# Two feed-forward blocks in two phases, with ten of eleven down units formed from seven products of block sums

## What is computed

```python
def swiglu(x, w1, w3, w2):
    return (jax.nn.silu(x @ w1) * (x @ w3)) @ w2

h = h + 0.5 * swiglu(rmsnorm(h, ffn1_norm[l]), ffn1_w1[l], ffn1_w3[l], ffn1_w2[l])   # FFN1
...   # pooling mixer and retention ("MIX", w_in, w_out)
h = h + 0.5 * swiglu(rmsnorm(h, ffn2_norm[l]), ffn2_w1[l], ffn2_w3[l], ffn2_w2[l])   # FFN2
```

## Time and profile before

| | us |
|---|---|
| three runs | 841.17, 840.43, 839.87 (median 840.43) |
| span of the profiled execution, first to last instruction | 837.8 |
| PE busy | 828.7 (99%) |
| DVE, ACT, POOL busy | 639.9, 447.6, 88.1 |

### The profile page before, as it was taken

One profiled execution on the slowest core, in us unless ns is written; L12 is line 12 of the kernel. 1 busy time (PEld: TensorE's weight loads), 2 busy tenths in 40 slices (PEclk: granted clock), 3 DMA queues, 4 the chain that ended last, 5 costly groups with the idle time before them and its releaser, 6 DMA issues.

```text
span 837.8 us, 13770 instructions
## 1 busy us (share of the span) xinstructions
PE 828.7 (99%) x5313; PEld 731.7 (87%) x5315; DVE 639.9 (76%) x791; ACT 447.6 (53%) x564; POOL 88.1 (11%) x93
## 2 busy tenths in 40 slices
PE   8999999999999999999999999999999999999996
PEld 6888888888988888888888899999998988888895
DVE  5786766667967587676667779897775898998897
ACT  6555444546324554544444756784425655665664
...
GB/s 242 317 240 210 184 196 205 167 201 159 243 158 144 151 206 259 239 180 197 204 194 169 132 220 156 132 172 223 159 154 198 141 201 201 150 200 212 189 175 51
DMA packets 119970, 157.73 MB, mean 188 GB/s; under 512 B 4429, under 2 KB 104173, under 8 KB 119805
## 3 DMA queue, kind: packets, MB, share of 16 engines
...
HBM read 154.42 MB, written 1.07 MB: 186 GB/s over the span
## 4 chain that ended last, share of the span: by engine, by line
PE 98%; DMA 1%; POOL 0%; ACTq 0%; DVE 0%; issue 0%; POOLq 0%; DVEq 0%
PE wk L1722 30%; PE acc L1844 20%; PE wk L1691 18%; PE wk L1730 16%; PE acc L1821 7%; PE wk L2171 1%; PE acc L2135 1%; PE acc L1738 1%; DMA x<-in_x 1%; PE acc L1691 1%; PE acc L2150 1%; PE wk L2233 1%; PE wk L2235 0%; PE acc L1857 0%; PE acc L2196 0%; PE wk L2031 0%
## 5 line engine op out<-in xcount | busy, mean ns | idle before, releaser
L1722 PE MATMUL wk<-xhl,w_hi 128*128 128x512 f32 x1104 | 268.9, 391 | 0.0
L1040 DVE TENSOR_TENSOR w_lo<-raw,w_hi 128x2048 fp32r<-128x2048 f32 x83 | 190.0, 2289 | 63.9 <-ACT w_hi L493 62.8
L1722 PEld LDWEIGHTS wk<-xhl,w_hi 128*128 128x128 f32 x1104 | 202.5, 188 | 38.9 <-issue 0.2
L493 ACT ACTIVATE w_hi<-raw 128x2048 fp32r<-128x2048 f32 x83 | 158.0, 1904 | 0.0
L1730 PEld LDWEIGHTS wk<-xhl,w_lo 128*128 128x128 f32 x1104 | 145.5, 191 | 8.0
L1730 PE MATMUL wk<-xhl,w_lo 128*128 128x256 f32 x1104 | 147.9, 282 | 0.0
L486 ACT ACTIVATE w_hi<-raw 128x2048 fp32r<-128x2048 f32 x55 | 104.6, 1910 | 51.6 <-PE wk L1691 29.9
L1023 DVE TENSOR_TENSOR w_lo<-raw,w_hi 128x2048 fp32r<-128x2048 f32 x48 | 110.2, 2300 | 21.3 <-ACT w_hi L486 21.1
L1844 PE MATMUL acc<-w_hi,hhl 128*128 128x512 f32 x480 | 119.4, 391 | 0.0
L1691 PE MATMUL wk<-xhl,w_hi 128*128 128x256 f32 x608 | 108.6, 286 | 0.0
L1844 PEld LDWEIGHTS acc<-w_hi,hhl 128*128 128x128 f32 x480 | 88.2, 188 | 17.1
...
## 6 DMA issues: line engine op xcount, KB each, us to landing
raw<-in_ffn_w SPq DMA_DIRECT2D x65, 1024.0 KB, 5.4
raw<-in_w_in SPq DMA_DIRECT2D x24, 1024.0 KB, 6.8
raw<-in_w_ffn_in SPq DMA_DIRECT2D x22, 1024.0 KB, 5.1
raw<-in_w_ffn_out SPq DMA_DIRECT2D x11, 1024.0 KB, 4.9
raw<-in_w_out SPq DMA_DIRECT2D x8, 1024.0 KB, 4.9
...
raw<-in_cmp_w_k SPq DMA_DIRECT2D x2, 1024.0 KB, 5.5
```

The costliest lines, as they stand in the source:

```text
L493: nc.scalar.activation(w_hi[:, s], raw[:, s], ACT.Copy).then_inc(hi_done, 1)
L1040: nc.vector.tensor_tensor(w_lo[:, s], raw[:, s], w_hi[:, s].bitcast(F32), ALU.subtract) \
L1722: mm = nc.tensor.matmul(bank, wh[:, c, cols], xhl[:, c].rearrange("p n t -> p (n t)"), start=c == 0, stop=False, skip_group_check=True)
```

## The change

FFN1 and FFN2 are done in two phases: first all 22 A and B units, then the 11 R units. The hidden values of ten steps are kept (`h_store`, in `arena`, and part of `mhl`) until then. The loops are written out.

For ten of the eleven R units the product of a 2 x 2 block of hidden values (two token tiles by two chunks of 128) and a 2 x 2 block of weights (two chunks by two halves of 512 columns) is formed from seven products of sums of blocks in place of eight products of blocks. Each of the seven has three passes of 512 columns, so PE does 21 matmuls in place of 24 for such a unit. They need four sums of hidden blocks for each step (`hidden_sums`: four POOL instructions of 128 x 128) and four sums of weight blocks for each unit (`folded_sums`: four POOL instructions of 128 x 512). The hidden store so has seven blocks in place of four: ACT and DVE cast and subtract 896 elements in place of 512. A unit's weights are seven blocks of 512 in place of four, in a ring of twelve (`ring_hi`, `ring_lo`): three blocks of the raw weights (`blocks_hi`, `blocks_lo`) and four sums (`sums_hi_part`, `sums_lo_part`, two at a time), 3584 elements in place of 2048 for ACT and for DVE. The sums of the units 2 and on lie where `xhl` lay, so POOL waits for the end of the first phase with them.

The seven products are summed over the units in seven or eight banks, four of `acc` and four of `wk`. At the end of the FFN they are combined (`folded_start` and `folded_corner` on DVE, three copies on ACT, two additions on POOL in `corner`). The gate's multiplication by `rstd_b` is left out; the per-token factor is put on at the end with `scale_t`. The loads of the MIX tables move from POOL's queue at the start to ACT's queue in the second phase, the bias loads on POOL and the clearing of `blk` (before FFN2) to the end of FFN2's sums.

```diff
+FB, RING = 512, 12
+FOLDED = FI - 1
+ITEMS = 7
+A_S1, A_S2, A_S3, A_S4, A_12, A_22, A_11 = range(ITEMS)
+PRODUCTS = ((A_12, 0), (A_S4, 2), (A_11, 4), (A_S3, 5), (A_S1, 6), (A_S2, 7), (A_22, 1))
+PAIRS = ((5, 6, 7, 2, 3, 4, 0, 1, 8, 9), (2, 0, 1, 3, 4, 5, 6, 7, 8, 9))
+IN_ARENA = 8
...
-        xhl = sb("xhl", [P, DC, 2, T], F32R)
+        xhl = nc.alloc_sbuf_tensor_at("xhl", [P, DC, 2, T], F32R, offset=XHL_AT)
+        sums_x23 = nc.alloc_sbuf_tensor_at("sums_x23", [P, 2, UNIT], F32, offset=XHL_AT)
...
+        weight_sums = [sqf, carve(56, UNIT), sums_x23[:, 0], sums_x23[:, 1]]
...
+
+        def h_pair(j):
+            return h_store[:, j] if j < IN_ARENA else mhl_pairs[:, j - IN_ARENA]
+
+        def product_bank(b):
+            return acc[:, b] if b < 4 else wk[:, b - 4]
...
+                if u is not None and sums_before(u):
+                    sp.wait_ge(w_sums, sums_before(u))
...
+                for p in range(FOLDED):
+                    j = PAIRS[f][p]
+                    unit(base + 2 * FI + p, r2[:, 2 * j:2 * j + 2, :], 2)
...
-                def h_hi(i, w2_before, dst=hh):
+                def h_hi(i):
                     act.wait_ge(h_out, i + (n0 + 1))
-                    if w2_before is not None:
-                        act.wait_ge(unit_done, w2_before)
-                    nc.scalar.activation(dst[:, 0:2], k_n(h_s, 2), ACT.Copy).then_inc(hh_out, 1)
-
-                a_part(0, base + 1)
+                    if i < FOLDED:
+                        act.wait_ge(h_sums, FOLDED * f + i + 1)
+                        nc.scalar.activation(h_pair(i)[:, 0], h_all[:, 0:ITEMS * P], ACT.Copy).then_inc(hh_out, 1)
+                    else:
+                        nc.scalar.activation(hh[:, 0:2], k_n(h_s, 2), ACT.Copy).then_inc(hh_out, 1)
...
+                def blocks_hi(p):
+
+                    u = base + 2 * FI + p
+                    act.wait_ge(raw_in[u % SLOTS], raw_count(u))
+                    ring_free(p, 2)
+                    for b, n, count in ring_parts(base, p, 0, 3):
+                        cast = nc.scalar.activation(ring_hi[:, b * FB:(b + count) * FB],
+                                                    raw[:, u % SLOTS, n * FB:(n + count) * FB], ACT.Copy)
+                    cast.then_inc(hi_done, 1)
+
+                def sums_hi_part(p, j):
+
+                    act.wait_ge(w_sums, 2 * (FOLDED * f + p) + j + 1)
+                    ring_free(p, 4 + 2 * j)
+                    for b, n, count in ring_parts(base, p, 3 + 2 * j, 2):
+                        cast = nc.scalar.activation(ring_hi[:, b * FB:(b + count) * FB],
+                                                    weight_sums[p % 4][:, (2 * j + n) * FB:(2 * j + n + count) * FB], ACT.Copy)
+                    cast.then_inc(sums_hi, 1)
...
+                h_hi(0)
+                for i in range(1, FI):
+                    a_part(i)
+                    if i < FI - 1:
+                        hi(base + 2 * i + 3)
+                    else:
+                        sums_hi_part(0, 0)
                     tanh(i)
-                    hi_in_loop(i, base, 2)
-                    b_part(i, i * 3 + (base + 1))
-                    hi_in_loop(i, base, 3)
-                    h_hi(i, i * 3 + (base + 2))
-                    hi_in_loop(i, base, 4)
-
-                a_part(FI - 1, base + 3 * FI - 3)
-                tanh(FI - 1)
+                    if i == FI - 1:
+                        sums_hi_part(0, 1)
+                    b_part(i)
+                    if i < FI - 2:
+                        hi(base + 2 * i + 4)
+                    else:
+                        blocks_hi(i - (FI - 2))
+                    h_hi(i)
+                for p in range(1, FOLDED):
+                    if p > 1:
+                        blocks_hi(p)
+                    sums_hi_part(p, 0)
+                    sums_hi_part(p, 1)
+                    if p == 5 and f == 0:
+                        act.wait_ge(unit_done, base + 2 * FI + 3)
+                        act.dma_start(table, a["c_table"]).then_inc(tables_in, 16)
+                        act.dma_start(pool_ws, a["pool_w"][0].rearrange("g k n -> k g n")).then_inc(tables_in, 16)
...
+            def hidden_sums(f, i):
+
+                s1, s2, s3, s4, a12, a22, a11, a21 = (h_all[:, n * P:(n + 1) * P] for n in range(8))
+                pool.wait_ge(h_out, FI * f + i + 1)
+                nc.gpsimd.tensor_tensor(s1, a21, a22, ALU.add).then_inc(pool_step, 1)
+                steps[0] += 1
+                summed = steps[0]
+                nc.gpsimd.tensor_tensor(s3, a21, a11, ALU.subtract).then_inc(pool_step, 1)
+                steps[0] += 1
+                pool.wait_ge(pool_step, summed)
+                step(nc.gpsimd.tensor_tensor(s2, s1, a11, ALU.subtract))
+                nc.gpsimd.tensor_tensor(s4, a12, s2, ALU.subtract).then_inc(h_sums, 1)
+
+            def folded_sums(f, base, p):
+
+                u = base + 2 * FI + p
+                b21, b22, b11, b12 = (raw[:, u % SLOTS, n * FB:(n + 1) * FB] for n in range(4))
+                t3, t1, t2, t4 = (weight_sums[p % 4][:, n * FB:(n + 1) * FB] for n in range(4))
+                pool.wait_ge(raw_in[u % SLOTS], raw_count(u))
+                if p == 2:
+                    pool.wait_ge(unit_done, base + 2 * FI)
+                if p >= 4:
+                    pool.wait_ge(sums_lo, 2 * (FOLDED * f + p - 3))
+                nc.gpsimd.tensor_tensor(t3, b12, b22, ALU.subtract)
+                nc.gpsimd.tensor_tensor(t1, b12, b11, ALU.subtract).then_inc(w_sums, 1)
+                pool.wait_ge(w_sums, 2 * (FOLDED * f + p) + 1)
+                step(nc.gpsimd.tensor_tensor(t2, b22, t1, ALU.subtract))
+                nc.gpsimd.tensor_tensor(t4, b21, t2, ALU.subtract).then_inc(w_sums, 1)
+
+            def folded_loop(f, base):
+
+                for i in range(FOLDED):
+                    hidden_sums(f, i)
+                    if i >= FOLDED - 2:
+                        folded_sums(f, base, i - FOLDED + 2)
+                for p in range(2, FOLDED):
+                    folded_sums(f, base, p)
+
+            def corner(f):
+
+                pool.wait_ge(corner_copied, 3 * f + 2)
+                step(nc.gpsimd.tensor_tensor(x_bank(3), x_bank(3), copy_5, ALU.add))
+                pool.wait_ge(corner_copied, 3 * f + 3)
+                nc.gpsimd.tensor_tensor(x_bank(3), x_bank(3), copy_3, ALU.add).then_inc(corner_added, 1)
...
+            def folded_start(f, base):
+
+                done = (ITEMS - 1) * (FOLDED * (f + 1) - 1)
+                dve.wait_ge(product_done, done + 3)
+                dve.wait_ge(corner_copied, 3 * f + 1)
+                step(nc.vector.scalar_tensor_tensor(out=x_bank(0), in0=product_bank(4), scalar=scale_t[:, 0:1], in1=x_bank(0),
+                                                    op0=ALU.mult, op1=ALU.add))
+                lo_first_half(base + 3 * FI)
+                dve.wait_ge(product_done, done + 6)
+                step(nc.vector.tensor_tensor(sum_2, product_bank(7), copy_1, ALU.add))
+                nc.vector.tensor_tensor(sum_3, product_bank(5), sum_2, ALU.add).then_inc(summed_3, 1)
+                dve.wait_ge(summed_3, f + 1)
+                step(nc.vector.scalar_tensor_tensor(out=x_bank(1), in0=sum_3, scalar=scale_t[:, 1:2], in1=x_bank(1),
+                                                    op0=ALU.mult, op1=ALU.add))
+
+            def folded_corner(f):
+
+                dve.wait_ge(corner_copied, 3 * f + 2)
+                step(nc.vector.tensor_tensor(sum_4, product_bank(6), sum_2, ALU.add))
+                step(nc.vector.scalar_tensor_tensor(out=x_bank(2), in0=sum_4, scalar=scale_t[:, 0:1], in1=x_bank(2),
+                                                    op0=ALU.mult, op1=ALU.add))
+
             def ffn(f, base, nstat):
                 n0 = FI * f
+
+                def blocks_lo(p):
+
+                    u = base + 2 * FI + p
+                    dve.wait_ge(hi_done, u + 1)
+                    for b, n, count in ring_parts(base, p, 0, 3):
+                        cols = slice(b * FB, (b + count) * FB)
+                        low = nc.vector.tensor_tensor(ring_lo[:, cols], raw[:, u % SLOTS, n * FB:(n + count) * FB],
+                                                      ring_hi[:, cols].bitcast(F32), ALU.subtract)
+                    low.then_inc(lo_done, 1)
+
+                def sums_lo_part(p, j):
+
+                    dve.wait_ge(sums_hi, 2 * (FOLDED * f + p) + j + 1)
+                    for b, n, count in ring_parts(base, p, 3 + 2 * j, 2):
+                        cols = slice(b * FB, (b + count) * FB)
+                        low = nc.vector.tensor_tensor(ring_lo[:, cols],
+                                                      weight_sums[p % 4][:, (2 * j + n) * FB:(2 * j + n + count) * FB],
+                                                      ring_hi[:, cols].bitcast(F32), ALU.subtract)
+                    low.then_inc(sums_lo, 1)
...
```

(89 more changed lines are left out.)

349 lines of the change are left out of this document (199 added, 150 removed).

## The result

| | us |
|---|---|
| changed kernel, median of 4 runs | 922.7 (921.2 to 924.9) |
| kernel before, median of 4 runs beside them | 840.2 (839.7 to 841.2) |
| ratio | 1.0988, 95% interval 1.0975 to 1.1002 |
| span of the profiled execution | 923.0 (before 837.8) |

The change costs 82.6 us. The forecast was 903, its range 875 to 938.

The account below looks back on a forecast made before the run. The port that DVE and POOL share was taken to bound the second phases: -13.7 (matmuls) + 57.2 (second phases) + 14.5 (first phases) + 5.0 (closing) = +63.0 on 840.4, so 903 us, range 875 to 938.

Parts of the forecast that it names:

- Direction and mechanism: Second phases: DVE and POOL take turns on a shared port, which bounds them; +28.6 us per FFN; slower at 92%.
- the signs that were named: Second phase: sums of 2 us and more, DVE and POOL alternating, PE waiting about 25 us per FFN, units 8 us apart.
- Matmuls: Ten units in each of two FFNs lose three matmuls on PE: 60 x 0.2275 = 13.7 us saved.
- Price of a unit on the port: Folded unit, second phase: 4.2 us of POOL sums plus 3.75 of DVE subtractions, 7.95 us against PE's 4.78.
- Backlog: Port work left when the second phase starts: 8.1 us of DVE items and 2.1 more, ahead of units 2 to 9.
- T: End of the last gate unit B10 on PE; unit 9 was forecast to end at T + 76.4.
- First phase: DVE steps of 11.5 us against PE's 11.11, unit 0's sums, A2 3.5 us late in FFN1; 14.5 us in all.
- Closing: End of each FFN: last low part 1.0 us late, transposes wait some 1.5; 5.0 us in all, 2 to 9.
- Moved at no cost: Moved table, bias and first-gain loads and blk clearing cost nothing; 1 to 4 us if any cover is missing.
- Side by side: Rival: DVE and POOL work at the same time, hidden beside PE's 4.78 us a unit; 831 us, chance 6%.
- short turns: Rival: second-phase port binds, but turns take 5.5 us a unit or less; 845 us at 5.5, chance 3%.
- The lower clock through the second phases: Rival: PE, waiting between bursts, is granted 1.2 GHz, a unit takes 9.55 us; 942 us, chance 9%.

Follow-up runs that it names:

- small_weight_sums: Changed kernel with POOL's four block sums of a folded unit cut from 512 columns to 8, other engines' instructions kept; 855.2 us, ratio to before 1.017.
- aligned: Changed kernel with xhl and the arena 32 bytes lower, both at a multiple of 64 bytes; 916.7 us, ratio to before 1.0903.

## Why the prediction was right, point by point

- **Direction and mechanism: right.** The port bounds the second phase. With narrow sums and every DVE instruction kept, the phase falls to PE's pace; with the sums on DVE it shortens although DVE does more. Of the signs that were named, sums of 2 us and more and the strict alternation came, and units 7.2 to 8.4 us apart; PE waited for DVE's low parts some 18 us in each FFN (19.8 + 15.5 over both), not 25, and more for raw blocks than for sums.
- **Matmuls: right.** PE has 60 fewer by the code; with the other causes gone they show as a gain. A folded unit takes PE 4.92 us in small_weight_sums, not 4.78, so part of the 13.7 us is lost again.
- **Price of a unit on the port: too low, by the sum's share.** I took 3.75 us for DVE and 1.05 for a sum in turn, 7.95 a unit, from rows of MIX. Measured from the end of the other engine's instruction to its own end, DVE's turns take 1.08 us for 1024 elements (174.33 to 175.41) and 1.61 for 1536 (169.34 to 170.95), 3.77 a unit, as taken. A sum's turn takes 1.15 (175.41 to 176.56), over both phases 1.12 to 1.16: the upper of my two rows held, and I had taken the middle. 3.77 + 4 x 1.15 = 8.37, as the stretches with four turns show. By "SBUF — State Buffer" of the Trainium skill, section "Who interferes with whom", the later instruction waits for the whole of the other, so that full lengths would add to an estimated 8.8 us. The trace agrees with the turns, but the instruction that has waited is shorter than alone (1.15 us for 1.30, 1.08 for 1.23), and 8.37 lies half way between 7.95 and 8.8. For units 2 to 9 the price makes 8 x 0.42 = 3.4 us.
- **Backlog: the order wrong, its size too small.** I put a backlog of 8.1 us of DVE's items ahead of units 2 to 9. In fact turns are one to one, a unit has three DVE instructions and four sums, and POOL had run ahead: DVE's items behind T took from 143.19 to 160.88, each with a POOL sum of unit 1, 2 or 3 ahead of it (a 512 subtraction 1.77 us, not 0.55), and units 2 to 9 came 7.2 to 8.4 us apart. That order alone adds nothing to the sum. What was missing in it is POOL's rest of unit 1: 3.7 us of port (to 143.69, and two sums more) where I had 2.1. With the price that is some 5 us: unit 9 ended at T + 81.2 and T + 81.5 for T + 76.4, 9.9 us too little in all.
- **First phase: the size right, the causes mixed.** DVE's steps of 11.53 us (forecast 11.5) and a wait of 3.25 us at A2 of FFN1 (forecast 3.5) came. The items named for A2 add up to 37.2, 4.0 us late, and not to 36.7, so that the 3.5 is a slip of the sum that lies nearer by luck. Units that are 0.1 us longer for their place pace PE at 11.31 a step, so less of the slack was DVE's to lose, and the clock that fell behind A2's wait, 5.44 - 3.89 = 1.55 us, was not in the sum.
- **Closing: right.** 1.21 us for the last low part in FFN1 and none in FFN2, 3.8 for the two transposes: 5.0, as forecast.
- **Moved at no cost: wrong.** I had named the cover (weights three slots ahead of units of 8 us) and priced its loss at 1 to 4 us, but taken it as holding. Five loads in a row hold the weight load behind them up for longer than that lead: 5.2 us.
- **Not seen at all: the place of the buffers,** 6.0 us by aligned. 9.9 + 5.2 + 6.0 = 21.1 us, against the 19.7 by which the forecast was low. That these three nearly close the gap is in part luck: the low clock behind single waits stands in none of the terms, and the place is partly covered by the first phases' own losses.
- **Rivals.** Side by side (831) and short turns fell with the traces; the terms named for short turns add up to 850 and not to 845, which changes nothing here. The lower clock through the second phases (942) did not come: 0.94 over the phase in FFN1 and in FFN2. It fell around single waits of 2 to 6 us, for 34 us in all. Where the waits are of 0.5 to 1.7 us, as in most units, it stayed at 2.4 GHz. "TensorE: Matmul & The Clock Gate" of the Trainium skill, section "HAM oscillation — how this bites in real kernels", by which a PE that waits between bursts can fall to the lower clock, agrees with the places where it fell.
